# Rotary turn by small row transfers instead of a TensorE product, in a hybrid decoder layer

## The reference

```python
proj = _rmsnorm(h, g_mix[i]) @ w_in[i]
def _partial_rope(x, pos):            # ROPE_DIM = 16, half = 8
    ang = pos.astype(jnp.float32)[..., None] * inv_freq
    cos, sin = jnp.cos(ang)[..., None, :], jnp.sin(ang)[..., None, :]
    x1, x2 = xf[..., :half], xf[..., half:ROPE_DIM]
    return jnp.concatenate([x1 * cos - x2 * sin, x2 * cos + x1 * sin, xf[..., ROPE_DIM:]], axis=-1)
```

## Time and profile before

| | us |
|---|---|
| median of 3 runs (lowest to highest) | 1541.29 (1541.25 to 1549.01) |
| the profiled execution, its time | 1538.67 |
| its span | 1536.8 |
| TensorE matmuls busy in the span | 1380.5 (90%) |
| VectorE busy | 760.4 (49%) |
| ScalarE busy | 628.8 (41%) |
| GpSimd busy | 166.6 (11%) |
| granted TensorE clock, mean | 0.947 |

### The profile page before, as it was taken

One profiled execution on the slowest core, in us unless ns is written; L12 is line 12 of the kernel. 1 busy time (PEld: TensorE's weight loads), 2 busy tenths in 40 slices (PEclk: granted clock), 3 DMA queues, 4 the chain that ended last, 5 costly groups with the idle time before them and its releaser, 6 DMA issues. The chain is left out here.

```text
span 1536.8 us, 24139 instructions
## 1 busy us (share of the span) xinstructions
PE 1380.5 (90%) x7980; PEld 1160.2 (75%) x7981; DVE 760.4 (49%) x1242; ACT 628.8 (41%) x932; POOL 166.6 (11%) x164
## 2 busy tenths in 40 slices
PE   5899999968999999999979973999999999938996
PEld 4677888957989998888858863777777787726774
DVE  5723112544444554344254335568755667846562
ACT  5212111213333333444353212567644656743442
POOL 2100000031111122223000000000000000011000
PEclk9999999979999999999979975999999999968998
DMA  7321321140010122353043214979976888784311
GB/s 248 83 82 55 110 87 56 30 110 22 23 35 22 35 48 45 87 135 85 1 126 109 97 55 150 357 250 379 399 269 232 298 331 318 299 315 142 134 63 41
DMA packets 107172, 221.44 MB, mean 144 GB/s; under 512 B 14525, under 2 KB 41197, under 8 KB 107094
## 3 DMA queue, kind: packets, MB, share of 16 engines
q1 hardware_dynamic: 95462, 178.87, 35.3%
q0 software_dynamic: 8608, 30.51, 5.8%
q10 hardware_dynamic: 3024, 11.01, 1.8%
HBM read 176.56 MB, written 36.24 MB: 138 GB/s over the span
## 5 line engine op out<-in xcount | busy, mean ns | idle before, releaser
L1256 ACT ACTIVATE att_prob<-att_ps_s 128x512 f32<-128x512 f32 (+1 forms) x240 | 134.6, 561 | 246.4 <-PE att_ps_s L1183 201.5
L1305 DVE TENSOR_REDUCE att_mx<-att_ps_m 128x1 f32<-128x512 f32 (+3 forms) x256 | 132.7, 560 | 134.5 <-PE att_ps_m L1130 122.8
L2031 DVE TENSOR_TENSOR exp_g_lo<-exp_g_raw,exp_g_hi 128x1024 fp32r<-128x1024 f32 x128 | 148.0, 1219 | 40.5 <-ACT exp_g_hi L1943 40.5
L136 PE MATMUL moe_ps_g<-exp_g_hi,moe_xT_hi 128*128 128x512 f32 x336 | 137.7, 410 | 13.9 <-DVE exp_g_lo L2031 13.8
L1943 ACT ACTIVATE exp_g_hi<-exp_g_raw 128x1024 fp32r<-128x1024 f32 x128 | 124.9, 1047 | 37.3 <-issue 19.2
L1201 PE MATMUL att_ps_o<-tok_vsw,att_prob 128*128 128x65 f32 x1056 | 140.1, 274 | 0.0
L137 PE MATMUL moe_ps_g<-exp_g_lo,moe_xT_hi 128*128 128x512 f32 x336 | 134.0, 399 | 0.0
L138 PE MATMUL moe_ps_g<-exp_g_hi,moe_xT_lo 128*128 128x512 f32 x336 | 133.9, 399 | 0.0
L1201 PEld LDWEIGHTS att_ps_o<-tok_vsw,att_prob 128*128 128x128 f32 x1056 | 131.2, 192 | 2.6 <-ACT att_prob L1256 0.5
L136 PE MATMUL prj_ps_w<-prj_hT_hi,prj_w_hi 128*128 128x512 f32 x256 | 103.0, 402 | 3.2 <-ACT prj_w_hi L416 1.7
L137 PE MATMUL prj_ps_w<-prj_hT_lo,prj_w_hi 128*128 128x512 f32 x256 | 101.2, 395 | 0.0
(11 more groups left out here) (358 smaller groups left out, 2965.4 us busy)
## 6 DMA issues: line engine op xcount, KB each, us to landing
exp_g_raw<-in_w_gate_e SPq DMA_DIRECT2D x128, 256.0 KB, 5.1
exp_g_raw<-in_w_up_e SPq DMA_DIRECT2D x128, 256.0 KB, 5.7
exp_d_raw<-in_w_down_e SPq DMA_DIRECT2D x64, 512.0 KB
y_rows<-moe_y ACTq DMA_DIRECT2D x21, 512.0 KB, 6.1
prj_w_raw<-in_w_in SPq DMA_DIRECT2D x16, 512.0 KB, 4.0
att_q_raw<-feat SPq DMA_DIRECT2D x32, 256.0 KB, 4.5
feat<-att_w_out POOLq DMA_DIRECT2D x14, 512.0 KB, 2.9
att_k_raw<-feat SPq DMA_DIRECT2D x24, 256.0 KB, 6.0
```

Of the source, the lines that this page charges most:

```text
L136: nc.tensor.matmul(out, a_hi, b_hi, start=first, stop=False)
L1256: nc.scalar.activation(prob[:, b % PT, 0:w], ps_s[:, b % ST, 0:w], ACT.Exp, scale=-1.0).then_inc(expd, 1)
L1305: last = nc.vector.tensor_reduce(mx[i % 2][:, col, q:q + 1], p[:, at:at + (kb - ka) * P], X, ALU.min)
L2031: nc.vector.tensor_tensor(g_lo[:, ch % GR], g_raw[:, ch], g_hi[:, ch % GR].bitcast(F32), ALU.subtract).then_inc(s_glo, 1)
```

## The change

The product with `K_ROT` goes from the turn of the blocks. In its place ScalarE issues four DMA transfers per block, behind its weight split: for each of the two heads, the rows of features 8 to 15 of `feat` go to rows 0 to 7 of a buffer `rot`, and rows 0 to 7 to rows 8 to 15. A transfer is 8 partitions of 4 KB. `rot` is the slot that held `gain`; VectorE clears it once, ahead of the angle tables, so that the rows that do not turn are 0. The sign moves from the matrix into the sine table, through a new column of constants, `K_SIGN`; the compressed keys are still turned by the matrix, now without its sign. VectorE turns a whole block with three operations of 1024 columns, and it makes the weight split of block n + 2 before them and no longer behind. ScalarE waits for the block before to be turned before it issues the transfers (`roped`), VectorE waits for the four to land (`rot_in`). `rope_nth(n)` is the number of turned blocks before n.

```diff
@@ -74,7 +74,8 @@
 K_TOK = K_COLS
 K_IOTA = K_TOK + NT
 K_ROW = K_IOTA + P
-K_COLS = K_ROW + 4
+K_SIGN = K_ROW + 4
+K_COLS = K_SIGN + 1
 HV = HD + 1
 R_MIN, R_CUM = HD, HD + 3
 
@@ -88,7 +89,7 @@
     rot = np.zeros((P, P), np.float32)
     for h in (0, HD):
         for d in range(ROPE_HALF):
-            rot[h + d + ROPE_HALF, h + d] = -1.0
+            rot[h + d + ROPE_HALF, h + d] = 1.0
             rot[h + d, h + d + ROPE_HALF] = 1.0
     c[:, K_ROT:K_ROT + P] = rot
     c[:, K_LT:K_LT + P] = (a[:, None] < a[None, :])
@@ -104,6 +105,7 @@
     rope = (a % HD) < 2 * ROPE_HALF
     c[:, K_FREQ] = np.where(rope, inv[a % ROPE_HALF], 0.0)
     c[:, K_ISROPE] = rope
+    c[:, K_SIGN] = np.where(a % HD < ROPE_HALF, -1.0, 1.0) * rope
     c[:, K_NOROPE] = ~rope
     c[:, K_VALID] = (a >= CMP_BLOCK - 1)
     c[:, K_PRI:K_PRI + 4] = np.arange(4, 0, -1)[None, :]
@@ -196,7 +198,7 @@
         w_hi = sc.sb("w_hi", [P, 2, KD, P], F32R)
         w_lo = sc.sb("w_lo", [P, 2, KD, P], F32R)
         feat = K["w_out"][:, 0:2, :]
-        turn = K["w_out"][:, 2, 0:S // 2]
+        rot = K["w_out"][:, 3, :]
         xt, gain = K["w_out"][:, 0:XR, :], K["w_out"][:, XR, :]
         cos_t = K["cos"]
         sin_t = K["sin"]
@@ -213,7 +215,6 @@
         v_lo = sc.sb("v_lo", [P, KD, VW], F32R)
         ps_x = sc.ps("ps_x", [P, 2, 512])
         ps_w = sc.ps("ps_w", [P, 2, 512])
-        ps_r = sc.ps("ps_r", [P, 512])
         ps_b = sc.ps("ps_b", [P, 512])
         ps_k = sc.ps("ps_k", [P, 512])
 
@@ -254,8 +255,8 @@
         rooted = sc.sem("rooted")
         var = sc.sem("var")
         w_in_ = [sc.sem(f"w_in{i}") for i in range(2)]
-        split_hi, split_lo, product, evac, rotated, turn_made = (
-            sc.sem(n) for n in ("split_hi", "split_lo", "product", "evac", "rotated", "turn_made"))
+        split_hi, split_lo, product, evac, rot_clear, rot_in = (
+            sc.sem(n) for n in ("split_hi", "split_lo", "product", "evac", "rot_clear", "rot_in"))
         roped = sc.sem("roped")
         stored = T["stored"]
         v_in = sc.sem("v_in")
@@ -279,6 +280,9 @@
         def stores_before(n):
 
             return sum(1 for m in range(n % 2, n, 2) if FIXED[m][1] is not None)
+
+        def rope_nth(n):
+            return sum(1 for m in range(n) if FIXED[m][2])
 
         VP = 4
         VK = KD // VP
@@ -365,13 +369,11 @@
                                            tokT[g * HD:(g + 1) * HD, kv, h]).then_inc(win_in, 16)
                 pool.wait_ge(win_in, 128)
                 pool.dma_start(w1[1], w1_d[1]).then_inc(w1_in, 16)
-                halves = 0
                 for n, (_, row, rope) in enumerate(FIXED):
                     if row is None:
                         continue
                     if rope:
-                        halves += 2
-                        pool.wait_ge(roped, halves)
+                        pool.wait_ge(roped, rope_nth(n) + 1)
                     pool.dma_start(T["feat"][row], feat[:, n % 2, :]).then_inc(stored[n % 2], 16)
                 with pool.Fori(0, NFIX // 2) as i:
                     for s in range(2):
@@ -440,6 +442,16 @@
                             copy_out(n % 2, h, 2 * n + h + 1, 16 * stores_before(n) or None,
                                      -SCALE if row < 4 else 1.0)
                     split((16 * (n // 2 + 2), 2 * n + 2 if n else 3), n % 2)
+                    if FIXED[n][2]:
+                        act.wait_ge(evac, 2 * n + 2)
+                        if rope_nth(n):
+                            act.wait_ge(roped, rope_nth(n))
+                        else:
+                            act.wait_ge(rot_clear, 1)
+                        for h in (0, HD):
+                            for to, at in ((h, h + ROPE_HALF), (h + ROPE_HALF, h)):
+                                act.dma_start(rot[to:to + ROPE_HALF, :], feat[at:at + ROPE_HALF, n % 2, :]
+                                              ).then_inc(rot_in, 16)
                     if n == 6:
                         act.wait_ge(bias_copied, 1)
                         for kv in range(2):
@@ -524,6 +536,8 @@
                     step(nc.vector.tensor_tensor(x, x, over, ALU.add))
                     step(nc.vector.tensor_scalar(x, x, 3.1415925, -3.1415925, ALU.min, ALU.max))
 
+                dve.wait_ge(scaled, NT)
+                nc.vector.memset(rot, 0.0).then_inc(rot_clear, 1)
                 dve.wait_ge(pos_in, 16)
                 dve.wait_ge(const_in, 32)
                 step(nc.vector.tensor_copy(ang, pos))
@@ -541,7 +555,7 @@
                 steps.inc(nc.vector.tensor_copy(K["maskb"][:], c[:, K_DIAG:K_DIAG + (2 + NT) * P]))
                 steps.inc(nc.vector.tensor_copy(K["identb"][:], c[:, K_ID:K_ID + P]))
                 dve.wait_ge(looked, 2)
-                step(nc.vector.tensor_scalar(K["sin"][:], K["sin"][:], c[:, K_ISROPE:K_ISROPE + 1], None, ALU.mult))
+                step(nc.vector.tensor_scalar(K["sin"][:], K["sin"][:], c[:, K_SIGN:K_SIGN + 1], None, ALU.mult))
                 step(nc.vector.tensor_scalar(K["cos"][:], K["cos"][:], c[:, K_ISROPE:K_ISROPE + 1],
                                              c[:, K_NOROPE:K_NOROPE + 1], ALU.mult, ALU.add))
                 cmp_ = Tally(own_cmp)
@@ -601,25 +615,19 @@
                     cmp_step(nc.vector.tensor_copy(K["kc_lo"][HD:P], c[HD:P, K_ROW + 2:K_ROW + 3].unsqueeze(2)
                                                    .to_broadcast((P - HD, GROUPS, P))))
 
-                halves = 0
                 for n, (_, _, rope) in enumerate(FIXED):
                     if n == NFIX - 1:
                         compressed_out()
-                    if rope:
-
-                        for h in range(2):
-                            halves += 1
-                            dve.wait_ge(rotated, halves)
-                            f = feat[:, n % 2, h * 512:(h + 1) * 512]
-                            nc.vector.tensor_tensor(turn, ps_r[:], sin_t[:, h * 512:(h + 1) * 512],
-                                                    ALU.mult).then_inc(turn_made, 1)
-                            own.inc(nc.vector.tensor_tensor(f, f, cos_t[:, h * 512:(h + 1) * 512], ALU.mult))
-                            own.wait(dve)
-                            dve.wait_ge(turn_made, halves)
-                            nc.vector.tensor_tensor(f, f, turn, ALU.add).then_inc(roped, 1)
-                            dve.wait_ge(roped, halves)
                     if n:
                         split(n % 2, n + 3)
+                    if rope:
+                        dve.wait_ge(rot_in, 64 * (rope_nth(n) + 1))
+                        f = feat[:, n % 2, :]
+                        own.inc(nc.vector.tensor_tensor(rot, rot, sin_t[:], ALU.mult))
+                        own.inc(nc.vector.tensor_tensor(f, f, cos_t[:], ALU.mult))
+                        own.wait(dve)
+                        nc.vector.tensor_tensor(f, f, rot, ALU.add).then_inc(roped, 1)
+                        dve.wait_ge(roped, rope_nth(n) + 1)
                     compress(n)
                 compressed_rope()
                 with dve.Fori(0, NFIX // 2 - 1) as i:
@@ -766,21 +774,10 @@
                                                 w2[:, 1, :], start=(g == 0), stop=(g == 1), skip_group_check=True)
                     last.then_inc(v_made, 1)
 
-                halves = 0
                 for n in range(2, NFIX):
-                    rope = FIXED[n][2]
                     block_of(n % 2, n + 1, 2 * n - 1)
                     if n == NFIX - 1:
                         compressed_out()
-                    if rope:
-                        for h in range(2):
-                            pe.wait_ge(evac, 2 * n + h + 1)
-                            if halves:
-                                pe.wait_ge(turn_made, halves)
-                            nc.tensor.matmul(ps_r[:], K["c"][:, K_ROT:K_ROT + P],
-                                             feat[:, n % 2, h * 512:(h + 1) * 512], start=True,
-                                             stop=True).then_inc(rotated, 1)
-                            halves += 1
                     compress(n)
                 pe.wait_ge(k_copied, 1)
                 nc.tensor.matmul(ps_k[:, 256:256 + N_CMP], K["c"][:, K_ROT:K_ROT + P], kc[:, 0:N_CMP], start=True,
```

## The result

The changed kernel took 1528.38 us in the median of 5 runs (1527.65 to 1532.91), the one before, in runs beside it, 1544.85 us (1541.25 to 1549.01). The ratio is 0.9909, with a 95% interval of 0.9889 to 0.9930: 14.1 us faster, by the interval 10.8 to 17.1 (the two medians alone are 16.5 us apart). The forecast was 1525.3 us, 16.0 us faster; 1528.38 is 3.1 us above it and inside its range. The forecast had started from a median of 1541.29 for the kernel before, which in these runs took 3.6 us more; in the gain itself forecast and measurement agree. The profiled execution took 1527.78 us.

A forecast was written before the change was run, and what follows sets the result against it. TensorE, busy for 90% of the span, was taken to bound the kernel. Gains of 1.9 (block 2), 11.4 (blocks 3 to 6) and 2.7 us (block 7) sum to 16.0, giving 1525.3 us, range 1521 to 1531.

The forecast's parts named there:

- What bounds the stage: Blocks with a turn: TensorE's own order is the longest chain; the turn costs 2.86 us of its time per block.
- Blocks 3 to 6, 11.4 us: Gaps after blocks 3 to 6: each gives 2.86 us once the turn products go, together 11.4 us.
- Block 2, 1.9 us: Gap after block 2: block 3 starts 2.73 us earlier, at 71.69, but a clock drop leaves 1.9 us gained.
- Block 7, 2.7 us: Gap after block 7: block 8 starts 2.7 us earlier; VectorE's copy is now bare for 0.1 to 0.2 us.
- The rows, covered: Row transfers: turn done 9.4 us after a block's end, costing 0 for landings up to 3.4 us.
- The estimate of 4.2 us for the landing: Row transfers serialized through two ports: some 2.4 us of moving plus 1.8, landing 4.2 us, sum 0.8 us smaller.
- rival 1: Turned blocks: rows come moderately late beside the weight load, TensorE waits 3.9 us, time 1529.2; chance 0.15 including smaller waits.
- The sum: Whole kernel: 1.9 + 11.4 + 2.7 = 16.0 us gained, no later stage changed.
- a later stage that grew: Stages after this one: growth in any would show the forecast wrong; the rest was to stay as long as before.
- Rival 3: Former turn gaps: TensorE finds another wait there; half remaining gives 1533, all 1539; chance 0.09 including a partly late chain.
- Rival 4: Block 3: the clock does not drop, 1.7 us more gained, 1523.6; chance 0.10.
- Rival 2: Turned blocks: rows so late they set the cycle, 25.1 us of waiting, 1550.4; chance 0.03 including another loss.

The follow-up runs named there:

- run 2: Changed kernel with the twelve turn products put back into TensorE's order, results unread and nobody waiting between the two of a block: 1536.4 us, ratio 0.9954 to the kernel before.
- run 7: Changed kernel with VectorE's order as before, the turn of block n first, then the lo weights of block n + 2: 1530.24 us, ratio 0.9907 to the kernel before.
- Run 6: Changed kernel with VectorE's lo weights for block 3 made ahead of its wait for the looked-up sine and cosine: 1524.86 us, ratio 0.9871 to the kernel before.
- run 3: Changed kernel with eight transfers of 4 rows a block instead of four of 8: 1531.28 us, ratio 0.9927 to the kernel before.
- run 4: Changed kernel with sixteen transfers of 2 rows a block instead of four of 8: 1540.06 us, ratio 0.9990 to the kernel before.
- run 5: The changed kernel again, unaltered, with a second profile: 1530.39 us, ratio 0.9905 to the kernel before.
- run 1: Kernel before, with only VectorE's lo weights of block n + 2 moved ahead of block n's turn, the turn staying on TensorE: 1563.0 us, ratio 1.0139.
- run 8: Run 6 plus ScalarE's hi half of the first value weights made during the last block, TensorE's wait there shortened: 1518.19 us, ratio 0.9834 to the kernel before.

## Why the prediction was right

- *What bounds the stage.* TensorE's order, shown by runs 2 and 7: putting its products back costs 7 to 8.6 us, putting VectorE's order back costs nothing.
- *Blocks 3 to 6, 11.4 us.* The four periods fell by 2.86, 2.86, 2.79 and 2.93 us, 11.4 in sum.
- *Block 2, 1.9 us.* 2.2 us, with the clock's fall as forecast. The forecast's start of block 3 (71.69) was 71.06: everything began 0.28 us earlier, VectorE's masking of the sine table took 0.76 us and not 1.05 (0.75 to 1.24 over the profiles), and the handover 0.1 us and not 0.15. Run 6 shows that the idle was there for these weights alone. The fall was the likelier case and not the sure one: run 3 has the same idle without it.
- *Block 7, 2.7 us.* 2.6 us (14.74 to 12.18), with the bare copy.
- *The rows, covered.* The turn was done at 8.8 us (9.4 forecast), by two errors that partly cancel: from one issue to the next it is 0.65 us and not about 0.5, but the first leaves 0.9 us sooner. The activations at block 6 had 1.4 us to spare (0.9 forecast). Run 3 used them up, run 4 made the cycle the rows' own. The estimate of 4.2 us for the landing (from the Trainium skill, SBUF — State Buffer, section "Door 1: The DMA port swizzle") was not borne out at blocks 3, 5, 6 and 7, where the rows are there at most 2.4 us after the last issue began; at blocks 2 and 4 it is 4.8 and 4.7, which is above the 2 to 4 us that I had named and a milder case of rival 1. That it fell on blocks where nothing waits was luck and not forecast: at block 6 the same delay would have cost about 0.9 us. The issues took 2.6 us and not 2.4.
- *The sum.* The stage's 16.0 was 16.2; the kernel's time moved by 14.1, with an interval that holds both. The prediction had named a later stage that grew as a sign of being wrong, and in the first profiles 5.2 us of the stage's gain are gone at the end. I took it that the later stages would take as long as before; between profiles of one code they differ by up to 8.6 us (run 5), in part because the same idle is followed by a fall of the clock in one and not in the other. The absolute time lay where I had put rival 1 and smaller waits (up to 1530), but none of them happened: the kernel before ran slower in these runs by 3.6 us.
- *The rivals.* Rival 3 (the gaps stay) is out by the period of 10.88 us behind blocks 3 and 6. Rival 4 (no fall of the clock at block 3) had a chance of 0.10 and came in one profile of five with that idle (run 3). Rival 2 was right in its mechanism. What I worked out from it for run 4 was too high: the cycle was 14.86 us and not 16.0, the wait for the activations 8.5 and not 15.4.

Open: why one issue of four takes 1.3 us after blocks 2 and 4, in both profiles of the changed kernel. Where it does, the last row issue is over after the weight load's has begun by 0.9 us or more, or begins after it, and the rows are there 2.3 to 3 us later. A load of the weights takes 4.0 us to land; counted from the issues at 97.84 and 72.16 that is 101.8 and 76.2, and the rows are there at 102.1 and 76.5. That they wait behind the load is the likely reading, and it isn't proven. Run 7, made for another purpose, supports it: there the weight load goes out 1.5 us ahead of block 4's first row issue, all four issues are short, and the rows are there 5.6 us after the block's end instead of 7.5. It wasn't tried further, since nothing waited for it.

## What to carry to other kernels

When the engine that sets the pace does a small job for another one, count the handover with it: here 1.85 us of products and 1.0 us of waiting per block, and both go when the rows are moved by DMA instead. A chain of small transfers was free here as long as issue, landing and use fitted into one period of the pace-setter; write that sum down, look for the one consumer that is due first, and look at what large transfer is issued beside the last small one. And an order that costs nothing after a change can be dear before it (runs 1 and 7), so its parts are not to be priced one by one in the old kernel.

## What the runs showed of the hardware

ScalarE's queue issues DMAs beside an activation that is still running: the first issue starts 0.14 us after the weight split of 1.05 us begins (84.36 and 84.50). An issue of a small transfer (8 rows of 4 KB, SBUF to SBUF) took 0.63 us there in the median of 24, and 1.25 to 1.35 in two of them, against 0.35 us for one of 512 KB to DRAM in the same queue; with 2 rows, sixteen issues a block, it is 0.57 us in the median. From the start of one issue to the next it is 0.65 us, and 0.60 to 0.64 with sixteen.

The same idle of 2.1 us ahead of the values, in the same place, left the clock at 1.00 in three profiles (before, runs 4 and 5) and was followed by a fall in the six others that have it. The changed kernel is in both groups, so the code doesn't decide it; what does isn't shown. With the idle closed (run 8) there was no fall there in its one profile.
